# Merge products of two attentions divided into parts that stay open in PSUM, and the rotary key in column groups

## What is computed

```python
proj = h @ p['w_in'][l]       # h: 640 x 1024, all branches from one projection
hy_in, da_q, da_k, da_v, mla_dq, mla_dkv, mla_kr, paths, merge = jnp.split(proj, IN_SPLITS, axis=-1)
y_hy  = hyena(...)                                   # branch 0
y_da  = differential attention, 4 heads              # branch 1
y_mla = latent attention, 8 heads; mla_kr is the one rotary key (32 rows) that all heads share
br = jnp.stack([y_hy, y_da, y_mla], axis=2) * jax.nn.silu(paths.reshape(b, n, N_BRANCH, BR_W))
y_br = jnp.einsum('blni,nid->blnd', br, p['w_branch'][l])
merged = jnp.sum(jax.nn.sigmoid(merge.reshape(b, n, N_BRANCH, D_MODEL)) * y_br, axis=2)
x = layer_norm(ALPHA * x + gate * (merged @ p['w_out'][l]), ...)
```

## Time and profile before

| | |
|---|---|
| median of 3 runs | 1870.74 us (1870.05 to 1871.19) |
| the profiled execution, whole | 1869.32 us |
| its span, first to last instruction | 1867.3 us |
| TensorE busy | 1777.1 us, 95% of the span |
| DVE, ACT, POOL busy | 1153.7, 681.9, 477.5 us |
| chain that ended last | PE 70%, DVE 17%, issue 5%, ACT 4% |
| mean granted TensorE clock | 0.987 of full speed |

### The profile page before, as it was taken

How to read it: one execution, slowest core, us unless ns; L and a number is a source line. 1 busy time by engine, 2 the same in 40 slices (tenths; PEclk the granted TensorE clock), 3 DMA queues, 4 the chain that set the end, 5 groups by cost and what they waited for, 6 DMA issues and landing times.

```text
span 1867.3 us, 28231 instructions
## 1 busy us (share of the span) xinstructions
PE 1777.1 (95%) x11464; PEld 1588.5 (85%) x11464; DVE 1153.7 (62%) x1620; ACT 681.9 (37%) x1174; POOL 477.5 (26%) x230
## 2 busy tenths in 40 slices
PE   5899999999999999999889999999999999999996
PEld 2888799878888888999877969998888888889996
DVE  5598894454464544576977989925544644435745
ACT  3424312444244544322273342224433454442122
POOL 0100033221241211467200000422223412125651
PEclk9999999999999999999999999999999999999998
DMA  9111122111211111354521112221112111115431
GB/s 357 46 57 35 34 91 74 51 51 55 68 35 56 45 39 50 136 192 136 229 91 35 57 34 70 78 68 40 55 57 68 37 46 53 43 46 184 139 113 62
DMA packets 50448, 150.04 MB, mean 80 GB/s; under 512 B 9674, under 2 KB 13898, under 8 KB 49552
## 3 DMA queue, kind: packets, MB, share of 16 engines
q1 hardware_dynamic: 46720, 134.09, 21.7%
q10 hardware_dynamic: 3600, 14.16, 2.2%
HBM read 141.63 MB, written 6.59 MB: 79 GB/s over the span
## 4 chain that ended last, share of the span: by engine, by line
PE 70%; DVE 17%; issue 5%; ACT 4%; DMA 2%; POOL 2%; SPq 0%; ACTq 0%; DVEq 0%; POOLq 0%
PE PS L835 16%; PE PS L836 15%; PE PS L840 15%; PE PS L907 4%; PE PS L896 3%; PE PS L1092 2%; PE PS L938 2%; PE PS L941 2%; PE PS L920 2%; DVE Wl L1577 1%; POOL Wl L2018 1%; DVE work L1550 1%; DVE work L1549 1%; DVE MG L1822 1%; ACT Wh L1215 1%
## 5 line engine op out<-in xcount | busy, mean ns | idle before, releaser
L2018 POOL TENSOR_TENSOR Wl<-W,Wh 128x1024 fp32r<-128x1024 f32 (+3 forms) x178 | 372.5, 2093 | 1227.5 <-ACT Wh L1215 1188.2
L835 PE MATMUL PS<-Hh,Wh 128*128 128x320 f32 x2048 | 613.2, 314 | 13.2 <-ACT Wh L1215 8.9
L836 PE MATMUL PS<-Hl,Wh 128*128 128x320 f32 x2048 | 605.1, 310 | 0.0
L835 PEld LDWEIGHTS PS<-Hh,Wh 128*128 128x128 f32 x2048 | 386.6, 189 | 36.7 <-issue 24.7
L836 PEld LDWEIGHTS PS<-Hl,Wh 128*128 128x128 f32 x2048 | 386.8, 189 | 0.2
L840 PE MATMUL PS<-Hh,Wl 128*128 128x320 f32 x2048 | 321.4, 309 | 0.6 <-POOL Wl L2018 0.6
L840 PEld LDWEIGHTS PS<-Hh,Wl 128*128 128x128 f32 x2048 | 305.5, 188 | 1.0 <-POOL Wl L2018 1.0
L1556 DVE TENSOR_REDUCE st<-PS 128x1 f32<-128x640 f32 (+1 forms) x160 | 114.9, 718 | 277.0 <-PE PS L920 155.9
L1215 ACT ACTIVATE work<-PS 128x640 f32<-128x640 f32 (+8 forms) x276 | 169.7, 624 | 227.2 <-PE PS L840 78.9
L1215 ACT ACTIVATE Wh<-W 128x1024 fp32r<-128x1024 f32 (+3 forms) x210 | 188.4, 900 | 64.0 <-PE PS L840 26.5
L1372 ACT ACTIVATE th<-PS 128x640 f32<-128x640 f32 x64 | 45.0, 703 | 341.2 <-PE PS L840 341.2
(11 more groups left out here) (253 smaller groups left out, 2592.8 us busy)
## 6 DMA issues: line engine op xcount, KB each, us to landing
W<-in_w_in SPq DMA_DIRECT2D x132, 512.0 KB, 3.5
W<-in_w_branch SPq DMA_DIRECT2D x48, 256.0 KB, 2.7
work<-in_w_mod_rows ACTq DMA_DIRECT2D x23, 512.0 KB, 4.1
pmod_w<-in_w_mod SPq DMA_DIRECT2D x8, 1024.0 KB, 11.2
W<-in_w_out SPq DMA_DIRECT2D x16, 512.0 KB, 4.5
work<-in_x_sample SPq DMA_DIRECT2D x2, 2048.0 KB
late_modulation_w<-in_w_mod_rows SPq DMA_DIRECT2D x5, 512.0 KB, 6.6
x_mid<-work SPq DMA_DIRECT2D x1, 2560.0 KB, 8.5
```

Of the source, the lines that this page charges most:

```text
L835: pe.matmul(out, Wh[:, b, kk, :], xh[:, kk, t], start=kk == 0, stop=False)
L836: pe.matmul(out, Wh[:, b, kk, :], xl[:, kk, t], start=False, stop=False)
L2018: return pool.tensor_tensor(out, in_, high.bitcast(f32), ALU.subtract)
```

## The change

A product in an attention is divided. A gate product becomes `mg0` (depth blocks 0 to 3 with the high weights, 16 matmuls), `mg1` (blocks 4 to 7, 16 matmuls) and `mgate` (the low weights, 16 matmuls). A branch product becomes `mb0` (16 matmuls) and `mbranch` (8). The first path product of branch 2 becomes `pa0`, `pa1`, `path` and stands at the end of the latent attention. The 40 parts of the 16 products stand two to a unit in `da` (one ahead of `ptrans`, one behind it) and one to a unit in `ml`. From its first part to its last a product keeps its PSUM tile; the other steps take turns in the three that are left, and the last part gives the tile back to the turn. A tile of weights belongs to the first part of its product. The rotary key is 64 fp32 matmuls of 32 weight columns and 160 tokens, four token quarters in four column groups of one PSUM tile; its weights aren't split, ScalarE and GpSimd copy one half of the 32 columns each. No other arithmetic changes.

```diff
+PARTS = {"mgate": ("mg0", "mg1"), "mbranch": ("mb0",), "path": ("pa0", "pa1")}
+BEGINS = {parts[0]: kind for kind, parts in PARTS.items()}
...
-        upto = min(t, 3) + 1 + 4 * h if full else len(fillers) * (u + 1) // len(units)
-        steps += fillers[taken:upto]
-        taken = upto
+        now, rest = rest[:each], rest[each:]
+        steps += now[:1]
         if u >= LAG:
             steps.append((tag + "_ptrans", u - LAG))
+        steps += now[1:]
...
+            begins = kind in BEGINS
+            kind = BEGINS.get(kind, kind)
+            if kind in ("mg1", "pa1") or held.pop((kind, i), None) is not None:
+                continue
             for j, (name, count) in enumerate(JOBS[kind](i)):
+                while at % SLOTS in held.values():
+                    at += 1
...
+                if begins:
+                    held[kind, i] = s
...
+                if part == 0:
+                    pe.wait_ge(*after("w_hi", l, n + 1))
+                    pe.wait_ge(*freed(l, kind, i))
+                if part < parts:
+                    for kk in range(4 * part, 4 * part + 4):
+                        for out, t in halves_of:
+                            pe.matmul(out, Wh[:, b, kk, :], xh[:, kk, t], start=kk == 0, stop=False)
+                            pe.matmul(out, Wh[:, b, kk, :], xl[:, kk, t], start=False, stop=False)
+                    return
...
+                quarters = [(ps[MR * j:MR * j + MR, 0:QUARTER], slice(QUARTER * j, QUARTER * j + QUARTER)) for j in range(4)]
...
+                    for x in (Hh, Hl):
+                        for out, t in quarters:
+                            last = pe.matmul(out, W32[:, b, kk, 0:MR], x[:, kk, t].bitcast(f32), start=kk == 0 and x is Hh,
+                                             stop=kk == KD - 1 and x is Hl)
```

More of the change, by code:

```diff
@@ L60, with in_parts, attention_steps @@
 LAG = 2
-def attention_steps(tag, heads, fillers, before=None, behind=None, full=False, cover=((), ())):
-    steps, units, taken = [], [(h, t) for h in range(heads) for t in range(NT)], 0
+PARTS = {"mgate": ("mg0", "mg1"), "mbranch": ("mb0",), "path": ("pa0", "pa1")}
+BEGINS = {parts[0]: kind for kind, parts in PARTS.items()}
+def in_parts(steps):
+    return [(kind, i) for step, i in steps for kind in PARTS[step] + (step,)]
+def attention_steps(tag, heads, parts, before=None, behind=None, early=0, cover=((), (), ())):
+    units = [(h, t) for h in range(heads) for t in range(NT)]
+    steps, rest, each = parts[:early], parts[early:], len(parts) // len(units)
     for u, (h, t) in enumerate(units):
@@ L181, in head @@
         return now + ([("mk", h // 2)] if t == NT - 1 and h % 2 == 0 else [])
-    s += [step for t in range(NT) for step in head(0, t)] + attention_steps("ml", MH, merge_steps(1), head)
+    last_path = in_parts(path_steps(2)[:1])
+    s += [step for t in range(NT) for step in head(0, t)]
+    s += attention_steps("ml", MH, in_parts(merge_steps(1)), head, early=1, cover=[[part] for part in last_path])
     mods = ModSteps(l)
     for c, step in enumerate(path_steps(2)):
-        s += [step] + ([("cload", 0)] if c == 0 else []) + mods.loads() + mods.take(MOD_PATH[l][c])
+        s += ([step] if c else [("cload", 0)]) + mods.loads() + mods.take(MOD_PATH[l][c])
     for d in range(KD):
@@ L222, in owned, with starts @@
     return [("out", i)] if kind in ("wo", "woa") else []
-STREAM = [(l, kind, i, key) for l in range(DEPTH) for kind, i in STEPS[l] for key in owned(kind, i)]
+def starts(l):
+    table = {}
+    for kind, i in STEPS[l]:
+        if kind in BEGINS:
+            table[kind, i] = (BEGINS[kind], i)
+        elif owned(kind, i) and (kind, i) not in table.values():
+            table[kind, i] = (kind, i)
+    return table
+STARTS = [starts(l) for l in range(DEPTH)]
+STREAM = [(l, *tile, key) for l in range(DEPTH) for tile in STARTS[l].values() for key in owned(*tile)]
 TILE_AT = {}
@@ L231 @@
 NP = 5
-SPLIT = [(kind, i) for kind, i in STEPS[0] if owned(kind, i)]
+SPLIT = list(STARTS[0].values())
+assert SPLIT == list(STARTS[1].values())
 NSPLIT = len(SPLIT)
@@ L790, in _ @@
                         norm_rows(l)
-                    for n in range(len(owned(kind, i))):
-                        if TILE_AT[l, kind, i] + n >= 2:
-                            weight(TILE_AT[l, kind, i] + n)
+                    tile = STARTS[l].get((kind, i))
+                    for n in range(len(owned(*tile)) if tile else 0):
+                        if TILE_AT[(l, *tile)] + n >= 2:
+                            weight(TILE_AT[(l, *tile)] + n)
                     if (kind, i) == ("conv", 2) and l == 0:
@@ L841, in project, with project_part @@
                 last.then_inc(full_of(l, kind, i), 1)
+            def project_part(l, kind, i, xh, xl, part):
+                n = SPLIT_AT[kind, i]
+                b, ps, k, parts = n % 2, slot(l, kind, i), depth(kind), len(PARTS[kind])
+                halves_of = [(ps[:, 512 * a:512 * a + HALF], slice(HALF * a, HALF * a + HALF)) for a in range(2)]
+                if part == 0:
[7 more added lines that the diff above has]
+                    return
+                pe.wait_ge(*after("w_lo", l, n + 1))
+                for kk in range(k):
+                    for out, t in halves_of:
+                        last = pe.matmul(out, Wl[:, b, kk, :], xh[:, kk, t], start=False, stop=kk == k - 1)
+                last.then_inc(full_of(l, kind, i), 1)
             def project_two(l, kk):
@@ L1424, in _ @@
                         act.wait_ge(*filled(l, kind, i))
-                        copy(halves(krs), two(slot(l, kind, i), p=MR)).then_inc(sems["kr_raw"], 1)
+                        for j in range(4):
+                            last = copy(krs[:, QUARTER * j:QUARTER * j + QUARTER], slot(l, kind, i)[MR * j:MR * j + MR, 0:QUARTER])
+                        last.then_inc(sems["kr_raw"], 1)
                     elif kind == "cc":
```

50 lines of the change are left out of this document (38 added, 12 removed).

## The result

The changed kernel takes 1905.43 us, median of 4 runs (1903.84 to 1906.57), beside 1870.39 us of the kernel before in the same comparison: 1.0196 times as long, 95% interval 1.0183 to 1.0208. It is 35 us slower.

What follows compares the result with a forecast made beforehand. TensorE, busy 95% of the span, was taken to bound the kernel. New waits 28.6 less 14.0 won give 14.6 us a layer, 29.2 in two; with 4.8 for the clock, 34 us more: 1903 us, range 1882 to 1923.

Steps and rivals of the forecast that it cites:

- 1: gates 2, 4, 6 and 1: Differential attention: the step behind each gate waits for ScalarE's tanh, 1.1 us for gates 2, 4, 6 and 0.9 for gate 1.
- 2: branches 2, 4, 6 behind `pv`: Differential attention: TensorE waits for VectorE's merge, held up by the head's copy and square; 1.64 us each, 4.9 for three.
- point 3: Differential attention, branch 0: VectorE does two maxima and the scaling before the merge; TensorE waits 3.1 us.
- Point 4: Latent attention, eight branches: maximum and scaling stand ahead of VectorE's merge; some 1.15 us each, 9.3 in all.
- point 5: Latent attention, gate 11: ScalarE stands at mqn 2's high part, delaying unit 14's transposes and mqn 2; 3.7 us.
- point 6: Path 9 waits 2.9 us for path 8's tile behind the last head's copies; 0.5 us at ml's first product.
- rotary key won: Rotary key: 48 matmuls, 7.05 us, become 16 groups of four, 4.4 us; 2.65 us won a layer.
- clock, both layers: Behind six new waits of 2.9 to 3.7 us: three half-speed stretches of some 1.6 us, 4.8 us in all.
- Tiles that come back at once: Both attentions: a closed product's tile goes to the next step, which waits for its reader; 28.6 us new waits a layer.
- The rival that ended faster: Better filling wins: 1855 us if VectorE reads branch products first, 1841 with no new wait; chance 0.09.
- the short waits: Rival: VectorE and ScalarE are idle each time; 6.9 us a layer, 1883 us, no clock loss; chance 0.17.
- The rival with long waits: VectorE's passes slower while GpSimd works, 0.7 us more on each of 12 waits; 1920 or 1926 us; chance 0.17.

Runs made afterwards that it cites:

- e1_turn: Changed kernel, but each step takes the PSUM tile given out or closed longest ago: 1845.58 us, -22.6 us against the kernel before.
- e9_skip_one: Changed kernel, but the very next step after a closed product may not take its tile: 1887.57 us, +18.7 us against the kernel before.
- e4_path_whole: Changed kernel, but path product 8 is whole and stands behind pv 7, as before the change: 1906.38 us, +38.2 us against the kernel before.
- e6_turn_high: e1_turn, with ScalarE making mqn 2's high part right behind gate product 11 and gate 8's ahead of mqn 0's copies: 1843.44 us, ratio 0.9865.
- e2_merge_first: Changed kernel, but VectorE scales a unit behind the merge pass, not ahead of it: 1899.70 us, +31.5 us against the kernel before.
- e11_turn_path_whole: e6_turn_high, but path product 8 whole behind pv 7: 1851.32 us, -17.5 us against the kernel before.
- e10_mqn_later: e1_turn, with mqn 1 to 3 one unit later and gate 8's high part as in e6_turn_high: 1852.68 us, -16.2 us against the kernel before.
- e3_high: Changed kernel, but ScalarE makes mqn 2's high part right behind gate product 11, ahead of its tanh: 1897.99 us, +29.8 us against the kernel before.
- e7_da_only: Changed kernel with parts in the differential attention alone; latent attention and path product 8 whole: 1894.83 us, +26.6 us against the kernel before.

## Why the prediction was right, step by step

| term, us a layer | predicted | measured |
|---|---|---|
| 1: gates 2, 4, 6 and 1 | 4.2 | 4.2 (3 x 1.12, 0.86) |
| 2: branches 2, 4, 6 behind `pv` | 4.9 | 5.0 |
| 3: branch 0 | 3.1 | 3.0 |
| 4: eight branches in the latent attention | 9.3 | 8.6 (8 x 1.07) |
| 5: `ptrans 14` and `mqn 2` | 3.7 | 3.6 (1.70, 1.94) |
| 6: path 9, first part of gate 8 | 3.4 | 3.6 (3.1, 0.5) |
| not named: parts of branches 3, 5, 7 | 0 | 1.6 (3 x 0.53) |
| old waits won | 11.3 | 11.1 |
| rotary key won | 2.65 | 2.8 |
| parts by themselves | 0 (0 to 4.8) | 0 in the differential attention, 0.5 in the latent (1.5 where its waits are gone) |
| clock, both layers | 4.8 | 5.8 (2.8 at path 9, 1.5 at each `mqn 2`) |

Without the parts' own cost these rows make 29.6 new, 13.9 won, 15.7 net, 31.4 in two layers, with the clock 37.2. The profiled executions differ by 37.2 us (1906.57 and 1869.32), the medians by 35.0. The forecast's 34 was right in mechanism and, but for one term, in its parts; that it lies within 1 us of the medians is partly luck, since both the waits and the clock were put too low. Old waits won are 0.2 short of 11.3, a gap that stayed at one part.

**Tiles that come back at once** was the cause. e1_turn and e9_skip_one show it by changing nothing else, and e9_skip_one took away exactly the two points whose tile went to the very next step. The waits were as long as forecast because each is a sum of durations that stood in the trace of before: what the reader still has ahead of it, up to the pass that frees the tile.

**The term that was missed.** The table of tiles ahead of the prediction listed the products with less than a whole `score` between. Branches 3, 5 and 7 begin behind the scores of a context block, which has 128 keys and takes a third of the time; the tanh of the gate before is not out of the tile, and each waits 0.53 us. "At least a whole `score`" was taken as cover without asking which.

**Point 4** was 0.08 us too long each, 0.7 in all. Maximum, scaling (two rows, the first at 596.53) and merge pass follow each other at 0.82 us on average, as put (595.68, 596.53, 597.32); only the allowance for signals was too wide.

**Points 5 and 6** were right as waits; the 3.7 us of point 5 are two waits, 1.70 and 1.94, with one transpose between. e4_path_whole shows that point 6 was not a loss by the division: the same parts save two waits ahead of `pv 7`, so undoing them wins 1.0 us of waits a layer, and in that run the clock took it.

**The rotary key** took 4.3 to 4.4 us. TensorE's timeline in the changed kernel, first and last of its 16 rows and what follows:

```profile
525.49 0.48 PE L934 MATMUL PS<-Hh,W 128*32 128x160 f32 x8
...
529.59 0.46 PE L934 MATMUL PS<-Hl,W 128*32 128x160 f32 x8
529.87 0.44 PE L959 MATMUL PS<-work,fixed 128*32 128x320 f32 x2
```

An fp32 matmul leaves two records here (64 matmuls, 128 records), so one row is one group of four: 0.27 us as taken, between the bounds from the earlier trace rows.

**The clock.** I took three half-speed stretches of 1.6 us out of six long waits. In the changed kernel the half-speed stretches behind `mqn 2` (layer 0, layer 1) and path 9 (layer 0), and last the window behind path 9 in layer 1:

```profile
663.30:666.70 3.40, 3.40 (x14) 3.40 (x14) 0.00 (x0) 0.00 (x0) 0.00 (x0) 0.50 0.09 34
1598.60:1602.00 3.40, 3.40 (x14) 3.40 (x14) 0.64 (x2) 0.00 (x0) 0.00 (x0) 0.50 0.26 107
782.80:789.60 6.80, 6.05 (x23) 6.08 (x24) 1.09 (x2) 0.90 (x1) 3.87 (x2) 0.50 0.90 347
1719.00:1725.80 6.80, 6.32 (x43) 6.35 (x44) 0.82 (x2) 0.00 (x0) 3.95 (x2) 1.00 0.51 183
```

Three stretches came, two behind waits of 1.9 us and one of double length behind the wait of 3.1; behind the same wait in layer 1 the clock stayed at its upper level. The number was right, by luck: nothing in the working says why three of six, and the same waits brought other numbers in other runs (below). The length of one was not right. The wait of 3.0 in the differential attention (point 3) brought none in this execution. The Trainium skill (TensorE: Matmul & The Clock Gate, Why this matters for your kernels) warns of longer gaps only; the trace differs, since a wait of 1.94 us at `mqn 2` went with 1.2 GHz in both layers.

**The rival that ended faster** (no new waits, 1841 us) described a kernel that the study then made: e6_turn_high, 24.8 us below the kernel before, where the rival's step was 28. What stood against it was the table of tiles alone.

**The bound of that rival and of the short waits** was put too high. By the terms given (a merge pass with 0.1 ahead and 0.14 behind it is 1.06 us, a tanh 0.94, less 0.55 where a `ptrans` lies between) points 1 to 4 add up to 11.5 us and not 13.8, with points 5 and 6 to 18.6, not 20.9: an estimate from the same rows. The short waits would then end at 1878 us, not at 1883. e2_merge_first shows that the bound was none: its eight waits of point 4 measure 0.59 us, where 0.7 was called the least. The forecast doesn't use the bound, and 18.6 is still above the 14.0 us that would have to be won back.

**The rival with long waits** falls: in the changed kernel all 32 merge passes of the two attentions (L1902 and L1905, both layers) took 0.82 us, eight of them while GpSimd was at work.

**Open:** why the clock falls behind one wait and not behind its twin. e4_path_whole and e11_turn_path_whole have the same steps at the end of the latent attention; `pv 7` ran at half speed in both layers of the one and in one layer of the other, and no run separates what comes before the wait from the wait.

## What to carry to other kernels

When a buffer is held open for longer, look at who gets it back, and when: write down for each release its next user, and compare the time to that user with the whole row of work that its reader still has ahead of it. A line in which a freed buffer goes to the end adds no instruction and was worth 58 us here. Take the short variant of each step as cover, not the usual one, and ask of each table of prefetches whether what it waits for is now open.

Short work between waits is worth more than its length: it hides several small waits at once, and where it is taken away the clock may take the gain.

## What was not expected of the hardware

Waits of TensorE of 1.0 to 3.1 us were followed by half speed, and not each time. In both layers: behind 1.3 us in e2_merge_first (`ptrans 37`), 1.8 us in e10_mqn_later (`pv 2`), 1.1 and 1.0 us in e4_path_whole (`pv 7`), 1.70 and 1.94 us in the changed kernel (`mqn 2`). In one layer of two: behind 2.0 and 1.0 us in e11_turn_path_whole and 3.1 us in the changed kernel (path 9). In neither: behind 1.7 us in e1_turn (`ptrans 14`) and 1.5 us in e3_high (`mqn 2`).

The wait of 3.0 us at point 3 kept the upper level in both layers of the changed kernel, but in e4_path_whole (layer 0) and in e7_da_only (layer 1) the same wait was followed by half speed. The window behind it in e4_path_whole, then in e7_da_only:

```profile
352.20:355.70 3.50, 3.50 (x14) 2.68 (x14) 0.00 (x0) 0.00 (x0) 0.00 (x0) 0.51 0.53 150
```

```profile
1278.00:1281.40 3.40, 3.40 (x14) 3.07 (x14) 0.00 (x0) 0.00 (x0) 0.00 (x0) 0.50 0.46 154
```

So the same instructions behind the same wait differ by 1.5 us or so from one execution to the next (169.2 and 169.1 against 167.6 in the table), and no single trace shows that a wait is safe. What undoing waits wins has to be read from medians: 1.0 us a layer fewer waits in e4_path_whole gave nothing.
